# GpSimd takes two of the eight chunks of the residual update of a 512-token stage, from an SBUF copy of the norm factor

## The chip, the cores and the metric

The kernel runs on one NeuronCore of a Trainium2 chip (trn2). The metric is the device time of one execution in microseconds, the median of several runs. The engines are named as the profile names them: PE is TensorE, DVE is VectorE, ACT is ScalarE, POOL is GpSimd, SP is SyncE.

## The reference: what is computed

The program is a stack of two models in fp32. The part that the change touches is the end of the two branches of the first model's first layer, where a branch's output y is normalised, scaled and added to the stream x. In NumPy form (the token dimension holds 256 context and 256 latent tokens, which have different gains):

```
y = branch(x)                      # hybrid attention, then the feed-forward net
f = 1 / sqrt(mean(y * y over the 1024 features) + eps)       # one factor per token
x = x + gain[feature, context or latent] * (y * f)           # residual
f2 = 1 / sqrt(mean(x * x) + eps)                             # the next norm follows at once
h = gain2 * (x * f2) + shift2                                # input of the next products
```

The gains and shifts are modulation values: they come from products of a condition vector with a large weight, `ada_w`, which is streamed and multiplied throughout the first model.

## The kernel before, in words

Features lie on the 128 partitions in eight chunks, and tokens along the free axis. So x and y are the SBUF tiles `X` and `Y` of [128, 8, 512], and one chunk is 128x512. The program is written engine by engine, each a fixed list of instructions with hand-placed semaphores; nothing reorders it.

Large products run on PE with every operand split into a high and a low part, three matmuls for one (L458 to L460). For that, ACT copies each weight slot into its high part (L385) and DVE subtracts to get the low part `w_lo` (L395).

The residual of a 512-token stage is done twice, at the end of the hybrid branch (r = 0) and of the feed-forward branch (r = 1). These are its steps.

- ACT squares the chunks of `Y` as they are finished (L1008), POOL adds the first six squares (`pool_y_sum`), and PE sums over the partitions (`pe_residual`).
- ACT takes the root (L1032), DVE the reciprocal (L1040), and PE spreads the result over all partitions into a PSUM bank, `wk[:, 1, :]` (L739). This is the factor f.
- `dve_residual`: for each of the eight chunks DVE makes `nt = Y * f` over 512 columns (L1055, `Y` from SBUF and the factor from PSUM). Then come two instructions of 256 columns, one for each kind of token, `X = nt * gain + X` (L1049, `nt` and `X` both from SBUF). The product of chunk c + 1 stands ahead of the update of chunk c.
- The next norm follows the chunks. ACT squares `X[c]` (L767) when chunk c is updated, and PE adds the squares (L734). In between, PE multiplies the streamed modulation weights (L551), and after the squares of chunks 3, 5 and 7 ACT issues the DMA for the ring slot that PE has used up (L572; the ring has three slots of 1 MB). After the eighth square come the root (L772), the reciprocal (L793), the spread (L739), and DVE's `nt = X * f2` (L809).
- Before ACT can make the first normed chunk (L782), it has to take over the row of modulation results (L569), for which PE must have multiplied the last ring slot (L551).

POOL has nothing to do from its last addition of squares to the feed-forward net's gating, where it multiplies (L1125, L1126) and subtracts (L1128) tiles of 128x512 in SBUF.

Of the kernel before, what the change touches and what calls it, by code (L numbers as in the profile page):

```python
# [20 lines left out]
ALU = mybir.AluOpType  # L21
ACT = mybir.ActivationFunctionType
AX = mybir.AxisListType

P = 128
D = 1024
DC = D // P
# [144 lines left out]
def stack_kernel(nc, t, out, layers):  # L172
# [3 lines left out]
    with ctx:  # L176
# [51 lines left out]
        nt = at("nt", [P, 2, T1], nt0 + 10 * KB)  # L228
        n32 = at("n32", [P, 2, T1], nt0 + 14 * KB)

        ada_first = [at(f"ada_first{i}", [P, SLOT], o) for i, o in enumerate(
# [87 lines left out]
        def sem(name):  # L319
            sems[name] = ctx.enter_context(nc.semaphore(name))  # L320
            return sems[name]
# [381 lines left out]
        mh_mul, mh_done = sem("mlp_products"), sem("mlp_hidden_done")  # L703
        x_ready = sem("x_ready")
        s_meta = sem("meta_loaded")

        def x_ready_for(eng, j, c):
            if j == 0:
                eng.wait_ge(s_x, 16)
            elif j <= 4:  # L710
                eng.wait_ge(x_ready, 8 * (j - 1) + c + 1)
            else:
                if j == 7:
                    if c % 4 < 2:
                        eng.wait_ge(x_ready, 4 * DC + c // 4 + 1)
                    else:
                        eng.wait_ge(freed["dve"], proj["c_outb"].freed0 + c // 4 + 1)
                    return
                p = proj[("ab_out1", "mlp0_out1", None, "mlp1_out1")[j - 5]]
                eng.wait_ge(freed["dve"], p.freed0 + c // p.C + 1)  # L720
            if j == 4:
                eng.wait_ge(s_meta, 5 * 16)
# [162 lines left out]

        s_sum, n32_ctx = sem("first_square_sum"), sem("norm_out_first_half")

        def pe_first_norm(pe):
            pe.wait_ge(s_const, N_CONST)
            pe.wait_ge(nsq_used, DC)  # L890
            pe.matmul(wk[:, 0, :], ones[:, :], sq_acc[:, :], start=True, stop=True).then_inc(s_sum, 1)

        def act_first_norm(act):
# [16 lines left out]
            for c in range(DC):  # L910
                if c >= 2:
                    act.wait_ge(nsq_used, max(c - 1, 2))
                act.activation(sq[:, c % 2, :], X[:, c, :], ACT.Square).then_inc(nsq_ready, 1)
            act.wait_ge(s_sum, 1)
            act.activation(root[:, :], wk[:, 0, :], ACT.Sqrt, bias=V("eps"), scale=1.0 / D).then_inc(root_ready, 1)
# [112 lines left out]
        def act_residual(act, r):  # L1028
# [3 lines left out]
            act.activation(root[:, 0:w], wk[:, 1, 0:w], ACT.Sqrt, bias=V("eps"), scale=1.0 / D).then_inc(yroot_ready, 1)  # L1032

        def dve_residual(dve, r):
            n, x0, groups, (layer, j), _ = RES[r]
            dve.wait_ge(s_gain, (5, 7, 8, 9)[r])
            dve.wait_ge(yroot_ready, r + 1)
            w = P if n == T1 else n
            by = wk[:, 1, 0:n] if n == T1 else rstd[:, 0:n]
            dve.reciprocal(rstd[:, 0:w], root[:, 0:w]).then_inc(yrstd_ready, 1)  # L1040
            if n == T1:
                dve.wait_ge(spread, 2 * r + 1)
            else:
                dve.wait_ge(yrstd_ready, r + 1)

            def update(c):
                dve.wait_ge(yt_ready, DC * r + c + 1)
                for s, a, b in groups:
                    ins = dve.scalar_tensor_tensor(X[:, c, x0 + a:x0 + b], nt[:, c % 2, a:b], gains[:, layer, j, s, c:c + 1],  # L1049
                                                   X[:, c, x0 + a:x0 + b], ALU.mult, ALU.add)  # L1050
                ins.then_inc(x_ready, 1)
            for c in range(DC):
                if c >= 2:
                    dve.wait_ge(x_ready, DC * r + c - 1)
                dve.tensor_tensor(nt[:, c % 2, 0:n], Y[:, c, 0:n], by, ALU.mult).then_inc(yt_ready, 1)  # L1055
                if c >= 1:
                    update(c - 1)
                if r == 3 and c >= 2:
                    dve_scaled(dve, 4, c - 2)
            update(DC - 1)  # L1060
            if r == 3:
                for c in (DC - 2, DC - 1):
                    dve_scaled(dve, 4, c)
# [1755 lines left out]
        def act_ffn(act, layer, r):  # L2819
# [13 lines left out]
            act_residual(act, r)  # L2833
            if layer == 0:
                act_ada(act, ADA_FIRST + ADA_LATE + 2, ADA_FIRST + ADA_LATE + 4)

# [15 lines left out]
        def pool_ffn(pool, layer, r):  # L2852
            if layer == 0:
                pool_ffn_in(pool, layer, 0)
                pool_ffn_in(pool, layer, 1)
            pool_y_sum(pool, r)

        def pe_ffn_halves(pe, layer, j):
# [43 lines left out]
        def _(act):  # L2902
# [8 lines left out]
            act_ada(act, ADA_FIRST + ADA_OUT, ADA_FIRST + ADA_OUT + 2)  # L2911
            act_residual(act, 0)
            act_ada(act, ADA_FIRST + ADA_OUT + 2, ADA_FIRST + ADA_OUT + 4)
            act_norm(act, 1, meanwhile=lambda: act_ada(act, ADA_FIRST + ADA_OUT + 7, ADA_FIRST + ADA_OUT + 9),
# [78 lines left out]
        def _(pool):  # L2993
# [3 lines left out]
            pool_rpb(pool, link)  # L2997
            pool_y_sum(pool, 0)
            pool_ffn(pool, 0, 1)
            pool_ret(pool)  # L3000
# [215 lines left out]
```

## Time and profile before

| | |
|---|---|
| median of 3 runs | 2021.95 us (2020.9 to 2023.43) |
| the profiled execution's own time | 2020.81 us |
| its span in the profile | 2019.1 us |
| PE busy | 1921.5 us (95%) |
| DVE busy | 1243.1 us (62%) |
| ACT busy | 920.0 us (46%) |
| POOL busy | 217.6 us (11%) |
| DVE, 273 to 286 us (first residual) | 11.31 us of 13 |
| DVE, 675 to 689 us (second residual) | 11.74 us of 14 |

The span runs from the first to the last instruction. The profiled execution took 1.7 us more than it, and the median of the runs lies 1.1 us above the profiled execution. A busy share is an average over stages: the two residuals together are a little over 1% of the time, and what limits them must be read there.

### The profile page before, as it was taken

Reading aid. Unit: us, or ns where it says so; the run is one execution under the profiler, and the core shown is the slowest. Engines: PE = TensorE matmul, PEld = TensorE weight load, DVE = VectorE, ACT = ScalarE, POOL = GpSimd, SP = SyncE. Lnnn points to the kernel's source line nnn. Section 1 sums busy time; section 2 is a strip of 40 time slices with the busy share of each in tenths; the row PEclk is TensorE's granted clock in tenths of the full one; section 3 lists DMA queues with packets and bytes.
Section 4 is the critical chain, followed back from the end, with each engine's and each line's share of the span. In section 5 each row is a group of like instructions: output and inputs, shape, how many; then the busy total and the mean of one; then the engine's idle time right before and its main releaser. Section 6 shows DMA issues by size and latency. Waiting matters only on the chain.

```text
span 2019.1 us, 33489 instructions
## 1 busy us (share of the span) xinstructions
PE 1921.5 (95%) x13389; PEld 1710.9 (85%) x13389; DVE 1243.1 (62%) x1853; ACT 920.0 (46%) x1438; POOL 217.6 (11%) x171
## 2 busy tenths in 40 slices
PE   4999989999999899999899998999999999989998
PEld 3776657778888589999889997998899999879997
DVE  6355455543564546577577767656975557787564
ACT  4344344322332522177465554357554444655353
POOL 2100104430552000011000000000000010000001
PEclk8999989999999899999989999999999999999999
DMA  8621465433223433222444553532345453225553
GB/s 358 247 78 63 149 247 179 169 114 112 99 75 107 167 125 108 102 84 84 167 158 167 198 178 126 177 134 87 127 171 184 167 179 135 95 95 181 185 177 125
DMA packets 43951, 296.79 MB, mean 147 GB/s; under 512 B 4976, under 2 KB 6128, under 8 KB 11696
## 3 DMA queue, kind: packets, MB, share of 16 engines
q1 hardware_dynamic: 36576, 247.48, 35.3%
q10 hardware_dynamic: 6048, 42.50, 5.8%
q0 software_dynamic: 1200, 5.02, 0.7%
q8 instruction: 91, 1.49, 0.3%
q14 instruction: 36, 0.29, 0.0%
HBM read 293.94 MB, written 1.05 MB: 146 GB/s over the span
## 4 chain that ended last, share of the span: by engine, by line
PE 84%; DVE 8%; ACT 4%; issue 1%; DMA 1%; POOL 1%; SPq 0%; ACTq 0%; DVEq 0%; POOLq 0%
PE acc L458 23%; PE acc L460 23%; PE acc L459 23%; DVE w_lo L395 2%; PE acc L453 2%; PE acc L455 2%; PE acc L454 2%; PE wk L551 1%; PE wk L1709 1%; DMA ada_first<-in_w_ada 1%; ACT w_hi L385 1%; PE acc L1698 1%; DVE X L1049 1%; PE wk L1438 1%; DVE nt L1055 1%
## 5 line engine op out<-in xcount | busy, mean ns | idle before, releaser
L395 DVE TENSOR_TENSOR w_lo<-w_raw,w_hi 128x1024 fp32r<-128x1024 f32 (+2 forms) x472 | 575.1, 1257 | 179.8 <-ACT w_hi L385 178.3
L458 PE MATMUL acc<-Hhi,w_hi 128*128 128x272 f32 (+2 forms) x2048 | 656.0, 320 | 24.8 <-DVE Hlo L804 7.6
L385 ACT ACTIVATE w_hi<-w_raw 128x1024 fp32r<-128x1024 f32 (+2 forms) x472 | 452.4, 1005 | 431.0 <-PE acc L460 346.4
L460 PE MATMUL acc<-Hhi,w_lo 128*128 128x272 f32 (+2 forms) x2048 | 637.9, 311 | 0.0
L459 PE MATMUL acc<-Hlo,w_hi 128*128 128x272 f32 (+2 forms) x2048 | 637.2, 311 | 0.0
L458 PEld LDWEIGHTS acc<-Hhi,w_hi 128*128 128x128 f32 x2048 | 388.6, 190 | 71.2 <-issue 38.7
L460 PEld LDWEIGHTS acc<-Hhi,w_lo 128*128 128x128 f32 x2048 | 388.4, 190 | 19.7
L459 PEld LDWEIGHTS acc<-Hlo,w_hi 128*128 128x128 f32 x2048 | 388.6, 190 | 18.0
L458 PE MATMUL acc<-Fhi,w_hi 128*128 128x256 f32 (+2 forms) x864 | 263.8, 305 | 3.0 <-POOL Flo L1128 1.5
L460 PE MATMUL acc<-Fhi,w_lo 128*128 128x256 f32 (+2 forms) x864 | 263.4, 305 | 0.0
L459 PE MATMUL acc<-Flo,w_hi 128*128 128x256 f32 (+2 forms) x864 | 263.1, 304 | 0.0
L458 PEld LDWEIGHTS acc<-Fhi,w_hi 128*128 128x128 f32 x864 | 162.4, 188 | 11.7 <-POOL Flo L1128 2.4
L460 PEld LDWEIGHTS acc<-Fhi,w_lo 128*128 128x128 f32 x864 | 162.5, 188 | 7.0
L459 PEld LDWEIGHTS acc<-Flo,w_hi 128*128 128x128 f32 x864 | 162.2, 188 | 6.6
L1084 ACT ACTIVATE cgu<-acc,vec 128x512 f32<-128x512 f32 x44 | 34.2, 779 | 125.6 <-PE acc L460 125.6
L1106 DVE SCALAR_TENSOR_TENSOR cgu<-acc,vec,cgu 128x510 f32<-128x510 f32 x44 | 32.6, 743 | 88.7 <-ACT cgu L1084 88.7
L458 PE MATMUL acc<-Rhi,w_hi 128*128 128x256 f32 (+1 forms) x256 | 84.3, 329 | 2.0 <-DVE Rlo L804 1.8
L460 PE MATMUL acc<-Rhi,w_lo 128*128 128x256 f32 (+1 forms) x256 | 79.3, 310 | 0.0
L459 PE MATMUL acc<-Rlo,w_hi 128*128 128x256 f32 (+1 forms) x256 | 79.2, 310 | 0.0
L453 PE MATMUL acc<-w_hi,Rhi 128*128 128x256 f32 x256 | 72.1, 282 | 0.0
L454 PE MATMUL acc<-w_lo,Rhi 128*128 128x256 f32 x256 | 70.7, 276 | 0.0
L455 PE MATMUL acc<-w_hi,Rlo 128*128 128x256 f32 x256 | 70.7, 276 | 0.0
(413 smaller groups left out, 2667.6 us busy)
## 6 DMA issues: line engine op xcount, KB each, us to landing
w_raw<-in_w_ffn_in SPq DMA_DIRECT2D x44, 1024.0 KB, 4.8
ada_ring<-in_w_ada ACTq DMA_DIRECT2D x40, 1024.0 KB, 6.0
w_raw<-in_w_mlp_in SPq DMA_DIRECT2D x32, 1024.0 KB, 4.8
w_raw<-in_w_mlp_out SPq DMA_DIRECT2D x32, 1024.0 KB, 4.8
w_raw<-in_w_ffn_out SPq DMA_DIRECT2D x32, 704.0 KB, 4.1
ada_first<-in_w_ada SPq DMA_DIRECT2D x8, 1024.0 KB, 18.2
w_raw<-in_w_ret_v SPq DMA_DIRECT2D x8, 1024.0 KB, 4.8
w_raw<-in_w_ret_g SPq DMA_DIRECT2D x8, 1024.0 KB, 4.8
```

The lines of the kernel that those rows point to most:

```text
L385: act.activation(w_hi[:, r, a:b], w_raw[:, r, a:b], ACT.Copy).then_inc(hi_done, 1)
L395: dve.tensor_tensor(w_lo[:, r, a:b], w_raw[:, r, a:b], w_hi[:, r, a:b].bitcast(F32), ALU.subtract).then_inc(lo_done, 1)
L453: pe.matmul(o, x_hi(k)[:, toks], w_hi[:, r, w], start=k == 0, stop=False)
L454: pe.matmul(o, x_hi(k)[:, toks], w_lo[:, r, w], start=False, stop=False)
L455: mm = pe.matmul(o, x_lo(k)[:, toks], w_hi[:, r, w], start=False, stop=k == last)
L458: pe.matmul(o, w_hi[:, r, w], x_hi(k), start=k == 0, stop=False)
L459: pe.matmul(o, w_hi[:, r, w], x_lo(k), start=False, stop=False)
L460: mm = pe.matmul(o, w_lo[:, r, w], x_hi(k), start=False, stop=k == last)
L551: mm = pe.matmul(wk[b:b + 32, bank, 0:256], cvec[:, k, 30 - 2 * j:62 - 2 * j], w[:, k * 256:(k + 1) * 256], start=first and k < 4, stop=la ...
L1049: ins = dve.scalar_tensor_tensor(X[:, c, x0 + a:x0 + b], nt[:, c % 2, a:b], gains[:, layer, j, s, c:c + 1], X[:, c, x0 + a:x0 + b], ALU.mu ...
L1084: act.activation(cgu[:, r, c, 0:n], acc_tile(p, r, c), ACT.Identity, bias=Vd("conv_b", m + layer * 44), scale=Vd("conv_w", m + (layer * 3 ...
L1106: dve.scalar_tensor_tensor(seqs(o, 1, SEQ), seqs(acc_tile(p, r, c), 0, SEQ - 1), w, seqs(o, 1, SEQ), ALU.mult, ALU.add).then_inc(conv_left, 1)
```

## The change

In both 512-token residuals, chunks 0 to 5 stay with DVE, and chunks 6 and 7 go to POOL. POOL has no path to PSUM in this program, so ACT first copies the factor from PSUM to a new SBUF tile `fac` (`act_factor`). DVE now reads `fac` too, not the PSUM bank. POOL does a chunk in four instructions: `nt_pool = Y * fac` over 512 columns, two products with the gains over 256 columns each, and `X = X + nt_pool` over 512 columns. The semaphore values that wait for an updated chunk are counted anew, since POOL's chunks report on a semaphore of their own. The 256-token residuals (r = 2, 3) stay as they were.

```diff
+        fac = at("fac", [P, T1], A + 20 * KB)
+        nt_pool = at("nt_pool", [P, 2, T1], A + 22 * KB)
...
+        POOL_C = (6, 7)
+        x_ready, pool_steps = sem("x_ready"), sem("first_sum_then_residual_steps_of_pool")
+        PER = 1 + 3 * len(POOL_C)
+        X_BASE = [0, DC - len(POOL_C), 2 * (DC - len(POOL_C)), 3 * DC - 2 * len(POOL_C), 4 * DC - 2 * len(POOL_C)]
...
             elif j <= 4:
-                eng.wait_ge(x_ready, 8 * (j - 1) + c + 1)
+                if j <= 2 and c in POOL_C:
+                    eng.wait_ge(pool_steps, PER * (j - 1) + 3 * POOL_C.index(c) + 5)
+                else:
+                    eng.wait_ge(x_ready, X_BASE[j - 1] + c + 1)
...
+        def act_factor(act, r):
+            act.wait_ge(spread, 2 * r + 1)
+            act.activation(fac[:, :], wk[:, 1, :], ACT.Copy).then_inc(pool_steps, 1)
+
+        def pool_residual(pool, r):
+            n, x0, groups, (layer, j), _ = RES[r]
+            pool.wait_ge(s_gain, (5, 7)[r])
+            pool.wait_ge(pool_steps, PER * r + 2)
+            for i, c in enumerate(POOL_C):
+                pool.tensor_tensor(nt_pool[:, i, :], Y[:, c, :], fac[:, :], ALU.mult).then_inc(pool_steps, 1)
+                pool.wait_ge(pool_steps, PER * r + 3 * i + 3)
+                for q, a, b in groups:
+                    ins = pool.tensor_scalar(nt_pool[:, i, a:b], nt_pool[:, i, a:b], gains[:, layer, j, q, c:c + 1], None, ALU.mult)
+                ins.then_inc(pool_steps, 1)
+                pool.wait_ge(pool_steps, PER * r + 3 * i + 4)
+                pool.tensor_tensor(X[:, c, :], X[:, c, :], nt_pool[:, i, :], ALU.add).then_inc(pool_steps, 1)
...
         def dve_residual(dve, r):
...
-            by = wk[:, 1, 0:n] if n == T1 else rstd[:, 0:n]
+            by = fac[:, 0:n] if n == T1 else rstd[:, 0:n]
             dve.reciprocal(rstd[:, 0:w], root[:, 0:w]).then_inc(yrstd_ready, 1)
             if n == T1:
-                dve.wait_ge(spread, 2 * r + 1)
+                dve.wait_ge(pool_steps, PER * r + 2)
...
-            for c in range(DC):
+            last = X_BASE[r + 1] - X_BASE[r]
+            for c in range(last):
...
-            update(DC - 1)
+            update(last - 1)
...
             act_residual(act, r)
             if layer == 0:
+                act_factor(act, 1)
                 act_ada(act, ADA_FIRST + ADA_LATE + 2, ADA_FIRST + ADA_LATE + 4)
...
             pool_y_sum(pool, r)
+            if r == 1:
+                pool_residual(pool, r)
...
             act_residual(act, 0)
+            act_factor(act, 0)
             act_ada(act, ADA_FIRST + ADA_OUT + 2, ADA_FIRST + ADA_OUT + 4)
...
             pool_y_sum(pool, 0)
+            pool_residual(pool, 0)
             pool_ffn(pool, 0, 1)
```

On POOL, at the end of the hybrid branch, the list of before goes from the sums of squares straight to the gating of the feed-forward net:

```order
L1018 TENSOR_TENSOR sq_acc<-sq_acc,sq 128x512 [waits y_square_added,y_square_ready] x5
L1125 TENSOR_TENSOR hid<-sg,cgu 128x512 [waits silu_done,acc_freed_dve]
L1126 TENSOR_TENSOR Fhi_100<-sg,cgu 128x512
L1128 TENSOR_TENSOR Flo_103<-hid,Fhi_100 128x512 [waits hidden_product]
L1125 TENSOR_TENSOR hid<-sg,cgu 128x512 [waits silu_done,acc_freed_dve]
```

After the change eight instructions stand there, whose inputs are all in SBUF:

```order
L1026 TENSOR_TENSOR sq_acc<-sq_acc,sq 128x512 [waits y_square_added,y_square_ready] x5
L1051 TENSOR_TENSOR nt_pool<-Y,fac 128x512 [waits first_sum_then_residual_steps_of_pool,gains_ready]
L1054 TENSOR_SCALAR nt_pool<-nt_pool,gains 128x256 [waits first_sum_then_residual_steps_of_pool]
L1054 TENSOR_SCALAR nt_pool<-nt_pool,gains 128x256
L1057 TENSOR_TENSOR X<-X,nt_pool 128x512 [waits first_sum_then_residual_steps_of_pool]
L1051 TENSOR_TENSOR nt_pool<-Y,fac 128x512
L1054 TENSOR_SCALAR nt_pool<-nt_pool,gains 128x256 [waits first_sum_then_residual_steps_of_pool]
L1054 TENSOR_SCALAR nt_pool<-nt_pool,gains 128x256
L1057 TENSOR_TENSOR X<-X,nt_pool 128x512 [waits first_sum_then_residual_steps_of_pool]
L1151 TENSOR_TENSOR hid<-sg,cgu 128x512 [waits silu_done,acc_freed_dve]
```

The five sums ahead and the gating behind are as they were.

On DVE, at the end of the same residual, this is the list of before (the products of chunks 6 and 7 with the updates of chunks 5 to 7, then the next norm's reciprocal):

```order
L1055 TENSOR_TENSOR nt<-Y,wk 128x512 [waits x_ready]
L1049 SCALAR_TENSOR_TENSOR X<-nt,gains,X 128x256 [waits y_scaled_ready]
L1049 SCALAR_TENSOR_TENSOR X<-nt,gains,X 128x256
L1055 TENSOR_TENSOR nt<-Y,wk 128x512 [waits x_ready]
L1049 SCALAR_TENSOR_TENSOR X<-nt,gains,X 128x256 [waits y_scaled_ready]
L1049 SCALAR_TENSOR_TENSOR X<-nt,gains,X 128x256
L1049 SCALAR_TENSOR_TENSOR X<-nt,gains,X 128x256 [waits y_scaled_ready]
L1049 SCALAR_TENSOR_TENSOR X<-nt,gains,X 128x256
L793 RECIPROCAL rstd<-root 128x128 [waits norm_root_ready]
```

And this is the list after the change, from the product of chunk 5 on:

```order
L1081 TENSOR_TENSOR nt<-Y,fac 128x512 [waits x_ready]
L1074 SCALAR_TENSOR_TENSOR X<-nt,gains,X 128x256 [waits y_scaled_ready]
L1074 SCALAR_TENSOR_TENSOR X<-nt,gains,X 128x256
L1074 SCALAR_TENSOR_TENSOR X<-nt,gains,X 128x256 [waits y_scaled_ready]
L1074 SCALAR_TENSOR_TENSOR X<-nt,gains,X 128x256
L801 RECIPROCAL rstd<-root 128x128 [waits norm_root_ready]
```

Two chunks (six instructions) are gone, and the second operand of every `nt` product is `fac` in SBUF where it was `wk` in PSUM.

On ACT, between the root of y and the squares of the next norm, the list of before is:

```order
L1032 ACTIVATE root<-wk,vec 128x128 [waits y_square_added]
L572 DMA ada_ring<-in_w_ada 128x2048 [waits ada_slot_used] x2
L767 ACTIVATE sq<-X 128x512 [waits x_ready] x2
L767 ACTIVATE sq<-X 128x512 [waits norm_square_summed,x_ready] x2
L572 DMA ada_ring<-in_w_ada 128x2048 [waits ada_slot_used]
```

After the change it is:

```order
L1040 ACTIVATE root<-wk,vec 128x128 [waits y_square_added]
L1044 ACTIVATE fac<-wk 128x512 [waits rstd_spread]
L574 DMA ada_ring<-in_w_ada 128x2048 [waits ada_slot_used] x2
L775 ACTIVATE sq<-X 128x512 [waits x_ready] x2
L775 ACTIVATE sq<-X 128x512 [waits norm_square_summed,x_ready] x2
L574 DMA ada_ring<-in_w_ada 128x2048 [waits ada_slot_used]
```

The copy of the factor stands ahead of two ring DMAs, and waits for PE's spread.

## Rows read from the trace of the kernel before

**Rows 1.** The page, part 4: the whole chain by engine.

```profile
PE 84%; DVE 8%; ACT 4%; issue 1%; DMA 1%; POOL 1%; SPq 0%; ACTq 0%; DVEq 0%; POOLq 0%
```

**Rows 2.** Chain of waits, first residual: start us, us, what.

```profile
272.57 1.29 DVE nt L1055 x2
...
282.25 0.69 DVE nt L1055
...
282.94 1.60 DVE X L1049 x4
...
285.24 0.47 PE wk L734 x8
...
285.73 0.38 ACT root L772
...
287.14 1.16 PE wk L739 x8
...
288.33 1.11 PE wk L551 x16
```

**Rows 3.** Timeline, first residual: start us, us, engine, line, op, names, [idle before].

```profile
269.31 0.33 ACTq L572 DMA_DIRECT2D ada_ring<-in_w_ada  x1
...
281.35 0.87 DVE L1049 SCALAR_TENSOR_TENSOR X<-nt,gains,X 128x256 f32<-128x256 f32 x2
...
282.26 0.33 ACTq L572 DMA_DIRECT2D ada_ring<-in_w_ada  x1
...
283.18 1.05 PE L551 MATMUL wk<-ada_ring,cvec 128*32 128x256 f32 x16
...
288.33 0.59 PEld L551 LDWEIGHTS wk<-ada_ring,cvec 128*32 128x32 f32 x16 [0.22 <-DMA ada_ring<-in_w_ada]
```

**Rows 4.** Timeline, second residual.

```profile
684.59 0.88 DVE L1049 SCALAR_TENSOR_TENSOR X<-nt,gains,X 128x256 f32<-128x256 f32 x2
...
685.58 0.34 ACTq L572 DMA_DIRECT2D ada_ring<-in_w_ada  x1
...
689.04 0.37 ACT L772 ACTIVATE root<-wk,vec 128x128 f32<-128x128 f32 x1 [0.61 <-PE wk L734]
...
691.53 1.07 PE L551 MATMUL wk<-ada_ring,cvec 128*32 128x256 f32 x16
```

**Rows 5.** Groups of instructions by line and shape: count, busy us, mean ns, idle.

```profile
L1125 POOL TENSOR_TENSOR hid<-sg,cgu 128x512 f32<-128x512 f32 x22 | 28.5, 1296 | 234.6 <-ACT sg L1088 234.6
...
L1018 POOL TENSOR_TENSOR sq_acc<-sq_acc,sq 128x256 f32<-128x256 f32 x10 | 7.4, 740 | 41.0 <-ACT sq L1008 41.0
...
L1015 POOL COPY sq_acc<-sq 128x256 f32<-128x256 f32 x2 | 0.8, 398 | 181.6 <-ACT sq L1008 181.6
...
L767 ACT ACTIVATE sq<-X 128x512 f32<-128x512 f32 x16 | 10.1, 630 | 19.8 <-DVE X L1049 14.5 <-PE wk L551 5.2
...
L1049 DVE SCALAR_TENSOR_TENSOR X<-nt,gains,X 128x256 f32<-128x256 f32 x48 | 21.4, 478 | 0.0
...
L1084 ACT ACTIVATE cgu<-acc,vec 128x512 f32<-128x512 f32 x44 | 34.2, 779 | 125.6 <-PE acc L460 125.6
```

**Rows 6.** Timelines: POOL and DVE in the feed-forward loop; DVE alone later.

```profile
333.44 1.31 POOL L1125 TENSOR_TENSOR hid<-sg,cgu 128x512 f32<-128x512 f32 x1 [6.53 <-ACT sg L1088]
...
334.70 2.27 POOL L1126 TENSOR_TENSOR Fhi<-sg,cgu 128x512 f32 x1
...
337.14 2.08 POOL L1128 TENSOR_TENSOR Flo<-hid,Fhi 128x512 f32 x1 [0.17 <-POOL Fhi L1126]
...
334.25 3.80 DVE L395 TENSOR_TENSOR w_lo<-w_raw,w_hi 128x1024 fp32r<-128x1024 f32 x2 [0.99 <-ACT w_hi L385]
...
1459.92 2.36 DVE L395 TENSOR_TENSOR w_lo<-w_raw,w_hi 128x1024 fp32r<-128x1024 f32 x2 [0.71 <-ACT w_hi L385]
```

**Rows 7.** Timelines: DVE and POOL in a later norm.

```profile
1822.92 4.79 DVE L834 SCALAR_TENSOR_TENSOR Hlo<-X,vec,Hhi 128x256 fp32r<-128x256 f32 x7
...
1823.37 3.66 POOL L845 TENSOR_TENSOR sq_acc<-sq_acc,sq 128x256 f32<-128x256 f32 x4 [0.59 <-ACT sq L828]
```

More of the change, by code:

```diff
@@ L703, in stack_kernel @@
         mh_mul, mh_done = sem("mlp_products"), sem("mlp_hidden_done")
-        x_ready = sem("x_ready")
+        POOL_C = (6, 7)
+        x_ready, pool_steps = sem("x_ready"), sem("first_sum_then_residual_steps_of_pool")
+        PER = 1 + 3 * len(POOL_C)
+        X_BASE = [0, DC - len(POOL_C), 2 * (DC - len(POOL_C)), 3 * DC - 2 * len(POOL_C), 4 * DC - 2 * len(POOL_C)]
         s_meta = sem("meta_loaded")
@@ L714, in x_ready_for @@
                     if c % 4 < 2:
-                        eng.wait_ge(x_ready, 4 * DC + c // 4 + 1)
+                        eng.wait_ge(x_ready, X_BASE[4] + c // 4 + 1)
                     else:
@@ L884, in final_norm @@
                         .then_inc(mh_done if by_pool else n32_ready, 1)
-        s_sum, n32_ctx = sem("first_square_sum"), sem("norm_out_first_half")
+        n32_ctx = sem("norm_out_first_half")
         def pe_first_norm(pe):
@@ L890, in pe_first_norm @@
             pe.wait_ge(nsq_used, DC)
-            pe.matmul(wk[:, 0, :], ones[:, :], sq_acc[:, :], start=True, stop=True).then_inc(s_sum, 1)
+            pe.matmul(wk[:, 0, :], ones[:, :], sq_acc[:, :], start=True, stop=True).then_inc(pool_steps, 1)
         def act_first_norm(act):
@@ L913, in act_first_norm @@
                 act.activation(sq[:, c % 2, :], X[:, c, :], ACT.Square).then_inc(nsq_ready, 1)
-            act.wait_ge(s_sum, 1)
+            act.wait_ge(pool_steps, 1)
             act.activation(root[:, :], wk[:, 0, :], ACT.Sqrt, bias=V("eps"), scale=1.0 / D).then_inc(root_ready, 1)
@@ L1046, in update @@
             def update(c):
-                dve.wait_ge(yt_ready, DC * r + c + 1)
+                dve.wait_ge(yt_ready, X_BASE[r] + c + 1)
                 for s, a, b in groups:
@@ L1051, in update @@
                 ins.then_inc(x_ready, 1)
-            for c in range(DC):
+            last = X_BASE[r + 1] - X_BASE[r]
+            for c in range(last):
                 if c >= 2:
-                    dve.wait_ge(x_ready, DC * r + c - 1)
+                    dve.wait_ge(x_ready, X_BASE[r] + c - 1)
                 dve.tensor_tensor(nt[:, c % 2, 0:n], Y[:, c, 0:n], by, ALU.mult).then_inc(yt_ready, 1)
```

## The prediction

> **What bounds the kernel now.** I read the page's chain first: PE holds 84% of it, DVE 8% and ACT 4% [rows 1]. An average over 2 ms says nothing on a step of 12 us, so next came the chain of waits in the first residual. There DVE holds it alone, from the first product at 272.57 to the last update at 284.54, in steps of one product (0.69) and two updates (0.80 together), about 1.5 us a chunk. After the last update come one square, one sum (285.24), the root (285.73), the reciprocal and spread (287.14 to 288.30), and then modulation products of PE at 288.33 [rows 2]. Third, the timeline: those products did not start by themselves. Their weights came from a ring DMA issued at 282.26, right when ACT squared chunk 5, and PE's weight load shows the DMA as its releaser at 288.33 [rows 3]. So two chains end together at 288.3: the residual's, and a DMA that starts when chunk 5 is updated. In the second residual the same two are there: chunk 5 updated at 685.47, DMA issued at 685.58, root at 689.04, products at 691.53 without a DMA wait [rows 4].
>
> I name the time at which chunk 5 is updated T5: 281.35 + 0.87 = 282.22 before.
>
> **What the change removes.** DVE loses two chunks, 3.0 us. Only the product of chunk 6 (0.69) stood ahead of T5; the rest (2.3) stood behind it. What now follows T5: PE's modulation products end 2.0 behind it (283.18 + 1.05 against 282.22 [rows 3]), and the two last sums need 0.47 each [rows 2]. They can't start before, since PE runs in order. So the root comes at T5 + 2.9, where it came at T5 + 3.5 (285.73). Of 3.0 us removed, 0.6 plus the 0.69 can be had.
>
> **What it adds ahead of DVE.** DVE now waits for ACT's copy of the factor, 128x512. A square of that size from SBUF takes 0.630, an instruction with scale and bias from PSUM 0.779 [rows 5]; I take 0.65 with the hand-over, near the plain one, which eats the 0.69. At the upper bound both residuals are 0.13 later. DVE's first product starts at 273.2. Six chunks alone take 282.22 - 272.57 - 0.69 = 9.0, so T5 without any disturbance is 282.2, as before.
>
> ACT's copy also holds back the ring DMA of 269.31 [rows 3] by about 3.9 us, to 273.2. With the 6.07 us from issue to use of the row at 282.26 it is there by 279.3; its slot is multiplied behind chunk 3, two chunks (3.0) ahead of 283.18, at 280.2 or later. Hidden by 0.9 us; if that cover fails, PE is late by what is missing. Behind DVE's and POOL's new waits nothing else is queued that could have run: POOL's next work is the gating, some 20 us later.
>
> **What POOL costs.** Per residual it does four instructions of 128x512 with two tensor inputs, and four products of 128x256 with one tensor input and a gain. The first kind takes 1.296 alone, 1.26 from start to start [rows 5, 6]. The second kind is not in this trace. Its bounds are a copy of 128x256 (0.398) and a two-input instruction of that size (0.740) [rows 5]; it has one tensor input, so I take 0.45, near the copy. Alone POOL needs 4 x 1.26 + 4 x 0.45 + 0.3 for its own waits = 7.1 us. It would be done at 280.4, well ahead of ACT's need for chunk 6.
>
> The Trainium skill, GPSIMD Engine Reference, section Engine selection, says that one-input elementwise work is roughly at line rate on GpSimd and two-input work about twice as slow as on VectorE. By it the gain product would be the copy's, and the sum below 0.4 us lower over both residuals; no run here shows it yet.
>
> **What the two engines do to each other.** This is the term that decides. In the feed-forward loop POOL's three instructions, 1.3 each, took 1.31, 2.27 and 2.08 when DVE's pair of `w_lo` subtractions (both inputs in SBUF) fell among them, and that pair took 3.80, where the same pair alone takes 2.36 [rows 6]. Both sides lost: DVE 1.44. They took turns: what DVE lost is the rest of `hid` (334.25 to 334.74, 0.49) and all of `Fhi` (1.25), less 0.1 at each of three changes of turn. The updates of the residual are of another opcode, so I looked for one of its form. In a later norm seven such (SBUF, pointer, SBUF, 128x256) took 4.79 while POOL added squares [rows 7]. Alone they take 6 x 0.40 + 0.48 = 2.9 [rows 2, 5]. DVE lost 1.9 to four POOL instructions of 0.740, 0.48 each: again the length less about 0.25. So each POOL instruction costs a busy DVE its own length less 0.2.
>
> Before the change the product took its factor from PSUM. Now `nt = Y * fac` has both inputs in SBUF, the form of `w_lo`, and the updates have the form just seen. Every DVE instruction of the residual can lose its turn, and DVE has 18 without a gap against POOL's 8. Loss: 4 x (1.26 - 0.2) + 4 x (0.45 - 0.2) = 5.2 us per residual. Bounds: with 0.4 instead of 0.2 for the turn, 4 x 0.86 + 4 x 0.05 = 3.6; with nothing for it and 0.740 for the products, 4 x 1.26 + 4 x 0.74 = 8.0.
>
> The Trainium skill, SBUF — State Buffer, section SBUF: two separate sides, calls the pair of ports that VectorE and GpSimd share an exclusive lock, taken by whichever starts first for the whole instruction, for VectorE instructions with two SBUF inputs as well. The trace agrees but for the 0.1 at each change of turn. With whole instructions the loss would be 4 x 1.296 + 4 x 0.45 = 7.0 and not 5.2.
>
> **The sum.** T5 becomes 282.2 + 5.2 = 287.4. POOL, with a DVE instruction between any two of its own, ends at about 283, so ACT doesn't wait for chunks 6 and 7. Root: 287.4 + 2.9 = 290.3, which is 4.6 later. The spread ends 2.57 behind it, at 292.9. The ring DMA is issued at 287.4 and with the same 6.07 is there at 293.5, 5.2 later than before; it may land sooner than before, with less behind it in the queue, so I take the middle, +4.9. Second residual: T5 690.7, root 693.6, +4.6, and its DMA had at most 5.95 (685.58 to 691.53), so it stays near the spread. Together +9.5 us: 2020.81 + 9.5 = 2030.3. The median of the runs lies 1.1 above the profiled execution, so I predict 2031. From the bounds: 3.6 gives 2 x 3.0 = +6.0 (2028 as a median), 8.0 gives about 2 x 7.6 = +15.2 (2037).
>
> **Rivals.**
> - *No collision.* T5 stays 282.2, POOL ends at 280.4. The root comes 0.6 earlier, but the ring DMA still leaves at 282.3 and is there at 288.3, so the first residual gains nothing; the second gains 0.6 at most. Median 2021.3 to 2022: no change. It decides if this DVE form doesn't give way to POOL. For it: no row has this very pair of instructions. Against it: [rows 6, 7] have both forms losing. Chance 0.1.
> - *POOL starves.* DVE keeps its turn from one instruction to the next, T5 is 282.2 and POOL does its 7.1 us behind it, to 289.3. Then a square and a sum (0.63 + 0.47): root 290.4, +4.7 each, the DMA hidden. 2020.8 + 9.4, as a median 2031. Against it: POOL got its turns in both rows. It is the same time with another picture. Chance 0.1.
> - *Whole instructions.* DVE loses 7.0, T5 is 289.2, root +6.4, the first DMA up to +7.0: about +13.1, median 2035. It is what the skill's rule gives. For it: POOL's 1.8 us lost in [rows 6] to two `w_lo` is nearly all of their 2.36. Chance 0.15.
> - *Faster after all.* Everything behind T5 moves freely and ACT's copy is hidden: 2 x 3.0 less 2 x 0.65, -4.7, median 2017. The ring DMA in [rows 3] speaks against it. Chance 0.02.
> - My forecast, +6 to +12: 0.6. The last 0.03 is left to a cover that fails (the held-back DMA), slower than all these.
>
> **How the numbers follow.** About 0.2% (4 us) is what a measurement of this kernel can tell from no change. Slower by more: forecast 0.6, starvation 0.1, whole instructions 0.15, the last 0.03, less 0.01 for a forecast that ends short: 0.87. Same: 0.11. Faster: 0.02. The time is that of the forecast, 2031. The range goes from 2027 (a little under the lower bound) to 2036, which takes in the rule's 2035 and leaves out the no-collision case.
>
> **What would show it.** Right: in the first residual `nt` products of DVE with a mean over 0.9 where they had 0.69, updates over 0.48 while POOL is busy, POOL's 128x512 over 1.6, T5 near 287, ACT idle ahead of the square of chunk 5 for DVE and not for POOL, root near 290. The time lost stands between 273 and 293 and again between 676 and 697, and nothing elsewhere. Wrong: DVE at its old lengths with POOL running beside it (no collision), or POOL's eight instructions behind DVE's last (starvation); a gain product on POOL over 0.74; or a slower stretch that neither residual holds.

## The result, and the profile after

The changed kernel takes 2031.71 us (median of 6 runs, 2027.89 to 2034.52); the kernel before takes 2023.05 us (6 runs, 2020.9 to 2024.35). The ratio is 1.0043, with a 95% interval of 1.0031 to 1.0056. That is 8.7 us slower (6.3 to 11.3). The forecast was 2031. Of all runs in this document one stands apart: one of the twelve runs of the kernel with POOL on two columns took 3812 us, and it is left out of that kernel's ratio.

The profiled execution after has a span of 2030.8 us, 11.7 more than the one before. Of these, 2.0 us were lost before the first residual, where no instruction of the engines' work is changed. The root of y comes at 271.89 there and at 269.90 before; in the ten other traces, with and without POOL's chunks, it comes at 269.66 to 271.45. So this part is spread between executions. The chain by engine is the same as in [rows 1], to the per cent, so the page doesn't show the loss. The chain of waits in the first residual shows it (start us, us, what):

```profile
274.56 0.61 ACT fac L1044
...
275.19 2.37 DVE nt L1081 x2
...
286.66 0.64 ACT sq L775
...
288.00 1.71 PE wk L553 x16
289.71 0.85 PE wk L742 x16
290.56 1.71 PE wk L553 x16
292.27 0.90 PE wk L742 x16
...
293.19 0.38 ACT root L780
...
295.75 1.04 PE wk L553 x16
```

Against [rows 2], ACT's copy of the factor has come into the chain. Two products of DVE that took 1.29 now take 2.37. And at the end the chain no longer runs through DVE's last update. It leaves DVE at the update of chunk 3, whose square starts at 286.66, and from 287.34 on it stays with PE, which needs 1.71 in the chain, twice, for modulation products between two sums. The timeline of the same stretch shows who ran beside whom (start us, us, engine, line, operation):

```profile
281.29 1.65 DVE L1081 TENSOR_TENSOR nt<-Y,fac 128x512 f32<-128x512 f32 x1
...
282.49 2.25 POOL L1054 TENSOR_SCALAR nt_pool<-nt_pool,gains 128x256 f32<-128x256 f32 x2
...
284.82 1.53 POOL L1057 TENSOR_TENSOR X<-X,nt_pool 128x512 f32<-128x512 f32 x1
...
286.66 0.69 DVE L1081 TENSOR_TENSOR nt<-Y,fac 128x512 f32<-128x512 f32 x1
...
287.27 1.67 DVE L1074 SCALAR_TENSOR_TENSOR X<-nt,gains,X 128x256 f32<-128x256 f32 x4
...
289.77 0.34 ACTq L574 DMA_DIRECT2D ada_ring<-in_w_ada  x1
...
290.33 1.93 PE L553 MATMUL wk<-ada_ring,cvec 128*32 128x256 f32 x16
```

POOL is done at 286.35, and DVE's next product is at once back at 0.69. Chunk 5 is updated at 288.94 (287.27 + 1.67). The modulation products of PE take 1.93, where [rows 3] had 1.05. The groups of the whole trace say how much longer each kind has become (count | busy us, mean ns | idle):

```profile
L1074 DVE SCALAR_TENSOR_TENSOR X<-nt,gains,X 128x256 f32<-128x256 f32 x40 | 22.8, 599 | 0.0
L1081 DVE TENSOR_TENSOR nt<-Y,fac 128x512 f32<-128x512 f32 x12 | 12.8, 1081 | 4.0 <-ACT fac L1044 3.8
...
L1054 POOL TENSOR_SCALAR nt_pool<-nt_pool,gains 128x256 f32<-128x256 f32 x8 | 9.0, 1133 | 0.4
...
L1051 POOL TENSOR_TENSOR nt_pool<-Y,fac 128x512 f32<-128x512 f32 x4 | 6.3, 1579 | 33.8 <-ACT fac L1044 33.8
L1057 POOL TENSOR_TENSOR X<-X,nt_pool 128x512 f32<-128x512 f32 x4 | 6.1, 1525 | 0.3
```

Both engines lost. The updates were 478 ns [rows 5] and the products 0.69 us [rows 2]. Per residual the loss is 40 x (0.599 - 0.478) / 2 = 2.4 us for the updates and 12 x (1.081 - 0.69) / 2 = 2.35 us for the products, 4.75 together. (The group of updates has in both kernels 16 instructions of the 256-token residuals, which are not changed; they drop out of the difference.)

This table splits each residual at the same marks, read from the timelines (us; first / second residual). "DVE" is from its first product to its last update, "tail" from there to the next norm's root, and "all" from the root of y to ACT taking over the modulation row, the last thing that the next stage needs.

| kernel | root of y to first product | DVE | tail | root to root | all |
|---|---|---|---|---|---|
| before (T5 at 9.65) | 2.67 | 11.96 / 11.95 | 1.20 / 1.27 | 15.83 / 15.89 | 19.57 / 19.57 |
| after | 3.30 | 13.75 / 13.74 | 4.25 / 3.29 | 21.30 / 20.33 | 24.93 / 24.01 |
| factor in PSUM | 3.30 | 11.38 / 11.37 | 3.46 / 3.58 | 18.14 / 18.25 | 21.77 / 21.93 |
| one after the other | 12.46 | 8.95 / 8.96 | 2.69 / 2.57 | 24.10 / 23.98 | 30.25 / 28.02 |
| POOL on 2 columns | 3.30 | 9.00 / 8.98 | 3.01 / 3.00 | 15.31 / 15.28 | 20.03 / 19.15 |
| gain products only | 3.30 | 9.70 / 9.71 | 2.51 / 2.79 | 15.51 / 15.80 | 20.80 / 19.60 |
| two-input ones only | 3.30 | 13.02 / 13.01 | 3.03 / 4.24 | 19.35 / 20.55 | 23.96 / 24.24 |
| one chunk | 3.30 | 12.92 / 12.91 | 1.73 / 1.79 | 17.95 / 18.00 | 22.46 / 21.68 |
| one chunk, PSUM | 3.30 | 10.96 / 10.96 | 1.72 / 1.79 | 15.98 / 16.05 | 20.52 / 19.73 |
| PE kept busy | 3.84 / 3.30 | 13.78 / 13.75 | 2.50 / 2.58 | 20.12 / 19.63 | 23.93 / 24.76 |
| ACT makes the gain product, first run | 2.67 | 10.44 / 10.44 | 1.21 / 1.27 | 14.32 / 14.39 | 24.01 / 18.07 |
| ACT makes the gain product, second run | 2.67 | 10.44 / 10.42 | 1.82 / 1.28 | 14.93 / 14.37 | 18.61 / 18.05 |

The two residuals cost 5.4 and 4.4 us more than before, 9.8 together. With the 2.0 of the opening, and -0.3 and +0.2 between and behind them, that is the 11.7 of the spans.

### The profile page after: what moved, and what is told of

It reads as the page before. It is cut to its first block, busy times and chain, and to the rows that moved or that the text cites. A ratio compares the mean times of both kernels' runs of the same rounds, so it can differ in the third digit from the quotient of the medians.

```text
span 2030.8 us, 33497 instructions
## 1 busy us (share of the span) xinstructions
PE 1925.7 (95%) x13389; PEld 1712.8 (84%) x13389; DVE 1248.0 (61%) x1841; ACT 920.8 (45%) x1440; POOL 237.9 (12%) x187
## 3 DMA queue, kind: packets, MB, share of 16 engines
HBM read 293.94 MB, written 1.05 MB: 145 GB/s over the span
## 4 chain that ended last, share of the span: by engine, by line
PE 84%; DVE 8%; ACT 4%; issue 1%; DMA 1%; POOL 1%; SPq 0%; ACTq 0%; DVEq 0%; POOLq 0%
PE acc L460 23%; PE acc L462 22%; PE acc L461 22%; PE acc L455 2%; DVE w_lo L397 2%; PE acc L457 2%; PE acc L456 2%; PE wk L553 2%; DMA ada_first<-in_w_ada 1%; PE wk L1735 1%; ACT w_hi L387 1%; PE acc L1724 1%; DVE nt L1081 1%; PE wk L1464 1%; DVE X L1074 1%
## 5 line engine op out<-in xcount | busy, mean ns | idle before, releaser
L460 PEld LDWEIGHTS acc<-Fhi,w_hi 128*128 128x128 f32 x864 | 162.3, 188 | 11.3 <-issue 2.2
```

Of the source, the lines that this page charges most:

```text
L460: pe.matmul(o, w_hi[:, r, w], x_hi(k), start=k == 0, stop=False)
```

## The experiments

Four questions were open: whether POOL and DVE really take turns and at what price for each kind of instruction; what the copy and the held-back DMA cost by themselves; why the tail is longer than forecast; and whether there is a form that wins.

**The factor from PSUM for DVE.** ACT still makes `fac`, and POOL reads it; DVE's products read the PSUM bank again.

```diff
-            by = fac[:, 0:n] if n == T1 else rstd[:, 0:n]
+            by = wk[:, 1, 0:n] if n == T1 else rstd[:, 0:n]
```

> DVE still waits for the copy of the factor, but its products read the factor from PSUM again, so only its updates have two SBUF inputs. Turns (my theory: an instruction of POOL and one of DVE with two SBUF inputs exclude each other): each of the products, 0.61 to 0.69 long, now runs beside POOL, so DVE loses less than the 4.75 us of the changed kernel. From the first product to the update of chunk 5 it takes about 12 us, not 13.75, all products have 0.69, and the time is some 3 us under the changed kernel, still 5 over the kernel before. Rival (any DVE instruction gives way to POOL, whatever it reads): 13.75 us again, products of 0.85 to 1.76, and the changed kernel's time. Rival (the copy and the ring DMA held back behind it cost the time, not the collisions): the changed kernel's time too, with short products.

Measured: 2027.9 us (before 2021.55), ratio 1.0034, 1.0021 to 1.0047. The groups of its trace:

```profile
L1074 DVE SCALAR_TENSOR_TENSOR X<-nt,gains,X 128x256 f32<-128x256 f32 x40 | 22.8, 599 | 0.0
...
L1081 DVE TENSOR_TENSOR nt<-Y,wk 128x512 f32<-128x512 f32 x12 | 8.1, 686 | 4.0 <-ACT fac L1044 3.8
L1054 POOL TENSOR_SCALAR nt_pool<-nt_pool,gains 128x256 f32<-128x256 f32 x8 | 8.0, 1005 | 0.4
```

The products are at 0.69 although POOL runs beside them, and the updates are as long as in the changed kernel. The loss of DVE is 11.38 - 9.0 = 2.4, the share of the updates alone. So the second input in SBUF is what makes a product give way to POOL, and half of the collision was brought in by `fac`. What keeps this kernel slower is the other half, the 0.63 of the copy, and a tail of 3.5.

**POOL on two columns.** All eight POOL instructions stay, each of two columns or one, and the rest of chunks 6 and 7 is not computed.

```diff
-                pool.tensor_tensor(nt_pool[:, i, :], Y[:, c, :], fac[:, :], ALU.mult)...
+                pool.tensor_tensor(nt_pool[:, i, 0:2], Y[:, c, 0:2], fac[:, 0:2], ALU.mult)...
-                for q, a, b in groups:
+                for q, a, b in [(1, 0, 1), (1, 1, 2)]:
-                pool.tensor_tensor(X[:, c, :], X[:, c, :], nt_pool[:, i, :], ALU.add)...
+                pool.tensor_tensor(X[:, c, 0:2], X[:, c, 0:2], nt_pool[:, i, 0:2], ALU.add)...
```

> POOL's instructions stay in number and order but work on two columns each, so most of the update of chunks 6 and 7 is left out. All waits, the copy of the factor and the held-back ring DMA stay. Turns: DVE is at its own speed, 9.0 us from the first product to the update of chunk 5 with at most 1 us lost to eight short POOL instructions; the root of the next norm comes 0 to 0.6 us earlier than before, and the time is that of the kernel before within 2 us (2021 to 2025). Rival (copy and held-back DMA cost the time): it stays 5 us or more above the kernel before, with PE waiting for the DMA.

Measured: 2021.86 us (before 2021.55), ratio 1.0001, 0.9992 to 1.0011. DVE takes 9.0 for six chunks, as read from [rows 2]: the collision is all of DVE's loss. But even here, with two chunks gone for nothing, the kernel is not faster. The root comes 0.5 earlier than before in the first residual, and the modulation row 0.46 later. PE's timeline there:

```profile
280.79 1.93 PE L553 MATMUL wk<-ada_ring,cvec 128*32 128x256 f32 x16
...
286.38 1.16 PE L747 MATMUL wk<-rstd,ident 128*128 128x128 f32 x8 [0.61 <-DVE rstd L801]
288.55 1.07 PE L553 MATMUL wk<-ada_ring,cvec 128*32 128x256 f32 x16 [1.01 <-DMA ada_ring<-in_w_ada]
```

PE stood 1.01 for the ring DMA, the second chain of [rows 3]. ACT issued that DMA at 282.79, not when chunk 5 was updated (281.96) but when the slot came free: PE's products of 280.79 took 1.93, at a granted clock of 0.61 in the mean from 280 to 284, and ended at 282.72. The second residual gains 0.4. Even so this tail is 3.0 where the kernel before had 1.2: the time that DVE saves is mostly spent behind it.

**Which POOL instructions cost what.** In one kernel only the gain products are whole, in the other only the two-input instructions; the others are cut to one or two columns.

```diff
 (gain products only; both two-input instructions cut to two columns as above)
-                    ins = pool.tensor_scalar(nt_pool[:, i, a:b], nt_pool[:, i, a:b], gains[...], None, ALU.mult)
+                    ins = pool.tensor_scalar(nt_pool[:, i, a:b], Y[:, c, a:b], gains[...], None, ALU.mult)
 (two-input ones only)
-                for q, a, b in groups:
+                for q, a, b in [(1, 0, 1), (1, 1, 2)]:
```

> The changed kernel with POOL's instructions of 128x512 cut to two columns and its gain products whole (most of the update of chunks 6 and 7 is left out). In e4 a gain product alone took 0.91 us, over my bound of 0.74, yet DVE lost only about 0.2 to each. If the hold on DVE is the reading of the tensor and not the length of the instruction, DVE loses 4 x 0.2 = 0.8 here: 9.8 us from the first product to its last update. Rival (a gain product holds DVE for its whole length): 4 x 0.9 = 3.6, so 12.6 us.

> The other half: POOL's four instructions of 128x512 with two inputs whole, the gain products on one column each (the gains of chunks 6 and 7 are left out). If each costs DVE 1.0 to 1.06, DVE loses 4.0 to 4.2: 13.0 to 13.2 us from the first product to its last update, where the changed kernel has 13.75. Rival (the loss goes with the count of POOL instructions and the turns between them): as in the changed kernel, 13.75.

Measured, one run each: 2026.23 and 2032.65 us. The times of single runs say little, the traces much. DVE and POOL with gain products only:

```profile
278.88 2.38 POOL L1054 TENSOR_SCALAR nt_pool<-Y,gains 128x256 f32<-128x256 f32 x2
...
279.37 1.09 DVE L1074 SCALAR_TENSOR_TENSOR X<-nt,gains,X 128x256 f32<-128x256 f32 x2
280.50 0.85 DVE L1081 TENSOR_TENSOR nt<-Y,fac 128x512 f32<-128x512 f32 x1
281.27 0.87 DVE L1074 SCALAR_TENSOR_TENSOR X<-nt,gains,X 128x256 f32<-128x256 f32 x2
```

Four gain products cost DVE 9.70 - 9.00 = 0.7, in steps of 0.22 (a pair of updates at 1.09 for 0.87) and 0.16 (a product at 0.85 for 0.69): 0.18 each, though each is 0.92 long alone and 1.17 beside DVE here. With the two-input instructions only:

```profile
276.94 0.88 DVE L1074 SCALAR_TENSOR_TENSOR X<-nt,gains,X 128x256 f32<-128x256 f32 x2
277.85 1.64 DVE L1081 TENSOR_TENSOR nt<-Y,fac 128x512 f32<-128x512 f32 x1
279.42 1.88 DVE L1074 SCALAR_TENSOR_TENSOR X<-nt,gains,X 128x256 f32<-128x256 f32 x2
```

Here a collision costs 0.95 to 1.01, and four of them 13.02 - 9.00 = 4.0. The sum of the parts, 4.7, is the 4.75 of the changed kernel.

**One after the other.** DVE begins only when POOL has finished both chunks.

```diff
-                dve.wait_ge(pool_steps, PER * r + 2)
+                dve.wait_ge(pool_steps, PER * r + 3 * len(POOL_C) + 2)
```

> DVE waits until POOL has done its two chunks, so neither disturbs the other: the price of each alone. POOL's instructions of 128x512 take 1.29 each, the gain products of 128x256 are near the copy's 0.40 (0.45 expected, 0.74 at most), together 7.1 us; then DVE's six chunks take 9.0 with products of 0.69, although they read both inputs from SBUF. If the products had over 0.8 here, the SBUF copy itself would be the slow source and not POOL. The update of chunk 5 comes at 16.1 us behind the copy, 2.4 later than in the changed kernel; with two residuals the time is about 2036.

Measured: 2041.74 us (one run). The groups:

```profile
L1081 DVE TENSOR_TENSOR nt<-Y,fac 128x512 f32<-128x512 f32 x12 | 8.1, 691 | 22.3 <-POOL X L1057 22.1
L1054 POOL TENSOR_SCALAR nt_pool<-nt_pool,gains 128x256 f32<-128x256 f32 x8 | 7.3, 921 | 0.4
...
L1051 POOL TENSOR_TENSOR nt_pool<-Y,fac 128x512 f32<-128x512 f32 x4 | 5.0, 1262 | 33.4 <-ACT fac L1044 33.4
L1057 POOL TENSOR_TENSOR X<-X,nt_pool 128x512 f32<-128x512 f32 x4 | 5.0, 1260 | 0.3
```

DVE's products with `fac` in SBUF are 0.69 when POOL is silent. POOL alone takes 9.0 us (274.12 to 283.14), not the 7.1 of the prediction. The 128x512 are 1.26 as forecast; the gain products are 0.92, where 0.45 was assumed. Those 1.9 us in each residual are most of what the run lies above its expectation.

**One chunk on POOL**, with the factor from SBUF and from PSUM.

```diff
-        POOL_C = (6, 7)
+        POOL_C = (7,)
 (the second kernel also)
-            by = fac[:, 0:n] if n == T1 else rstd[:, 0:n]
+            by = wk[:, 1, 0:n] if n == T1 else rstd[:, 0:n]
```

> POOL gets only chunk 7, DVE seven chunks. Turns: the loss goes with the number of POOL instructions, four and not eight, so DVE loses about 2.4 us per residual, and chunk 6 costs it 1.5 again. Update of chunk 5 at 9.65 + 2.4 = 12.05 us behind the first product, update of chunk 6 at 12.9; the root about 3 us later than before per residual, the time 5 to 6 us above the kernel before. Rival (a fixed cost of using POOL at all, as the copy, the wake-up or the DMA held back): the time of the changed kernel, 8 to 9 us above.

> The kindest form of the change: POOL has chunk 7 alone, and DVE's products read the factor from PSUM. By the turns DVE loses half of what e1 lost, 1.2 us, and has seven chunks: 10.5 + 1.2 = 11.7 us, from a start that is 0.63 later for ACT's copy. So DVE's end is 0.4 later than before, and ACT and PE follow it with less: from the root of y to the next row of modulation results 19.6 to 20.3 us, where before had 19.57; the time is 0 to 2 us over the kernel before, no change. If it were clearly faster, POOL could pay after all, and my reading that the copy and the turns eat all of it would be wrong.

Measured: 2027.13 us, ratio 1.003 (1.0018 to 1.0041), and 2023.61 us, ratio 1.0007 (0.9997 to 1.0017). With half the POOL instructions the loss up to chunk 5 is half, 12.1 - 9.65 = 2.5. With the factor in PSUM as well, DVE's seven chunks take 10.96 for 10.5 undisturbed, and the kernel can't be told from the one before. The expectation had a loss of 1.2, half of the 2.4 with two chunks, and 0.5 came. POOL's first product falls on DVE's products here as there, and they lose nothing. With one chunk its gain products cost 0.22 and its addition 0.30 (a pair of updates at 1.17 for 0.87). With two chunks and the factor in PSUM its first addition and its second product both fall on one pair of updates (2.19 for 0.87), and its last addition on the last four (2.37 for 1.67). So the price goes by which DVE instruction a POOL instruction meets, and not by the count of POOL's instructions alone. What is left to win goes to the ring DMA again: PE waited 0.83 for it in the first residual.

**PE kept busy.** In the changed kernel, six small products of no use stand ahead of the sums of chunks 0, 1 and 3, to see whether PE's idle time between chunks lengthens the tail.

```diff
+                if j in (1, 2) and c in (0, 1, 3):
+                    for _ in range(6):
+                        pe.matmul(acc[:, 0, 0:P], ones[:, :], ones[:, :], start=True, stop=True)
                 pe.wait_ge(nsq_ready, DC * j + c + 1)
```

> The changed kernel with six idle-time matmuls (ones by ones, 128 columns, into an unused PSUM tile) on PE ahead of the squares of chunks 0, 1 and 3 in both norms, where PE otherwise waits about 2 us for each chunk. In the changed kernel the next root comes 4.25 and 3.29 us behind DVE's last update, where I had 2.9, and the modulation products there take 1.93 and not 1.05. If that is PE at its lower clock after the idle waits (my theory), the products behind chunks 3 and 5 take 1.05 to 1.1, the root comes 2.7 to 3.0 us behind DVE's last update in both, DVE's 13.75 stays, and the time is 1 to 2 us under the changed kernel. Rival (the products wait for their weights or for ACT, not for the clock): they keep 1.93 or the root keeps its 4.25 and 3.29.

Measured: 2031.54 us (before 2022.86), ratio 1.0046, 1.0029 to 1.0062. The 1 to 2 us that were expected under the changed kernel did not come. The stretches of the first residual in the kernel before (PE, PEld, DVE, ACT and POOL busy, then PEclk, the granted clock; 1.00 is 2.4 GHz and 0.50 is 1.2 GHz):

```profile
276.00:280.00 4.00, 3.53 (x44) 1.68 (x48) 3.90 (x9) 1.99 (x4) 0.00 (x0) 0.51 0.84 317
280.00:284.00 4.00, 2.69 (x56) 1.33 (x56) 3.93 (x9) 1.50 (x3) 0.00 (x0) 1.00 0.93 317
```

in the changed kernel:

```profile
276.00:280.00 4.00, 1.92 (x24) 0.42 (x12) 3.96 (x6) 0.63 (x1) 3.81 (x4) 0.50 0.91 332
280.00:284.00 4.00, 2.03 (x24) 0.99 (x24) 3.93 (x5) 0.65 (x2) 3.90 (x4) 0.50 0.49 197
284.00:288.00 4.00, 1.65 (x24) 0.80 (x24) 3.96 (x6) 1.24 (x2) 2.26 (x2) 0.50 0.19 27
288.00:292.00 4.00, 4.00 (x48) 2.17 (x44) 0.94 (x3) 2.41 (x4) 0.00 (x0) 0.50 0.88 301
```

and with the filler:

```profile
280.00:284.00 4.00, 3.32 (x45) 2.24 (x44) 3.97 (x4) 0.63 (x1) 3.90 (x4) 0.98 0.59 244
284.00:288.00 4.00, 2.51 (x36) 2.04 (x40) 3.93 (x7) 1.26 (x2) 2.37 (x2) 1.00 0.26 39
288.00:292.00 4.00, 3.29 (x72) 1.73 (x68) 1.09 (x4) 2.78 (x5) 0.00 (x0) 1.00 0.85 348
```

The cause of the long tail is shown: the clock is at 0.98 to 1.00 from 280 on, the modulation products are back at 1.05, and the tail is 2.50 and 2.58 instead of 4.25 and 3.29. But only the first residual is shorter, by 1.0. (Its 3.84 to the first product is not the filler's: PE's spread, ahead of any filler, took 1.70 for 1.16.) In the second the root is 0.7 earlier and the modulation row 0.75 later. PE's timeline in the second residual:

```profile
699.17 1.07 PE L553 MATMUL wk<-ada_ring,cvec 128*32 128x256 f32 x16 [0.26 <-DMA ada_ring<-in_w_ada]
700.45 1.16 PE L747 MATMUL wk<-rstd,ident 128*128 128x128 f32 x8 [0.21 <-DVE rstd L804]
702.99 1.07 PE L553 MATMUL wk<-ada_ring,cvec 128*32 128x256 f32 x16 [1.38 <-DMA ada_ring<-in_w_ada]
```

The DMA was issued at 696.51, landed 6.4 later and was used 6.48 later. In the changed kernel the same DMA was issued at 698.07, landed 4.8 later, 0.2 ahead of its use, and held nothing up. So a shorter tail uncovers the DMA, as in the kernel with two columns, but that is not all of it: the DMA also took 1.6 longer. It was issued 2.31 behind the ring DMA before it, where the changed kernel had 3.10; whether that is the cause, no run shows.

**The gain product on ACT.** This one starts from the kernel before. ACT is idle while Y is finished, so it multiplies `Y` by the gain there, behind the squares, and the last chunks behind the root. DVE's update becomes one plain addition of 128x512, and POOL has no part in it.

```diff
+        def act_gain(act, r, m):
+            n, x0, groups, (layer, j), _ = RES[r]
+            act.wait_ge(ysq_ready, DC * r + m + 1)
+            for s, a, b in groups:
+                ins = act.activation(Y[:, m, a:b], Y[:, m, a:b], ACT.Identity, scale=gains[:, layer, j, s, m:m + 1])
+            ins.then_inc(y_gained, 1)
...
+                if r < 2:
+                    dve.tensor_tensor(X[:, c, :], X[:, c, :], nt[:, c % 2, :], ALU.add).then_inc(x_ready, 1)
+                    return
```

> From the kernel before, without POOL and without a copy of the factor: ACT multiplies each chunk of Y by its gain in place, behind its square, in time in which it is idle; DVE's residual is then nt = Y * f and one X = X + nt over 512 columns where it had two instructions of 256. If DVE's chain is what the residual lasts (my theory), a chunk takes 1.31 and not 1.51 us, eight chunks 10.4 and not 11.95, and from the root of y to the next row of modulation results it is about 18.1 us, not 19.57, in both residuals: 2.5 to 3 us less in all, some 0.13%, at the edge of what the runs can tell. Rival (the ring DMA that leaves when chunk 5 is updated sets the end): the first residual gains what chunk 5 gains, 1.1, the second 1.4. Rival (the longer ACT list delays the squares or the root): the stretch from Y to the root grows by 1 us or more and the gain is gone.

> The kernel of e5 once more, for one thing: in the profile of e5 PE waited 3.9 us in the first residual for a ring DMA, and the gain of 1.5 us in DVE's chain was lost there five-fold, though the median was 1.7 us better. If the wait is of one execution, this profile has about 18.1 to 18.5 us from the root of y to the modulation row in the first residual, as in the second, and the time is again some 0.1% under the kernel before. If the earlier chain always outruns the ring there, the wait of several us is here again.

Measured: 2020.16 us (before 2021.85), ratio 0.9989, 0.998 to 0.9997; and again 2021.82 us (before 2022.86), ratio 0.9992, 0.9982 to 1.0001. DVE's timeline in the second run:

```profile
281.28 0.68 DVE L1064 TENSOR_TENSOR X<-X,nt 128x512 f32<-128x512 f32 x1
282.00 0.69 DVE L1075 TENSOR_TENSOR nt<-Y,wk 128x512 f32<-128x512 f32 x1
282.61 1.29 DVE L1064 TENSOR_TENSOR X<-X,nt 128x512 f32<-128x512 f32 x2
```

One update takes 0.68, where the pair took 0.87 [rows 3], and all eight chunks 10.44 instead of 11.96. The residuals are 1.0 and 1.5 us shorter. In the profile of the first run PE stood 3.88 for the ring DMA in the first residual, which made that residual 4.4 us longer than before. The DMA issued at 279.95 took 8.9 us to land; in the repetition the same one, issued at 279.36, took 5.0 and PE didn't wait, so that stall belongs to one execution. Why it was slow there, the traces don't show. This kernel beats the changed one by about 10 us. Over the kernel before its gain is 1 to 2 us, at the edge of what the runs can tell.

## Why the prediction was right

- **What DVE loses to POOL.** Forecast 5.2 us per residual, measured 4.75. The mechanism is shown three ways: it is gone with two columns, half gone with half the instructions, and gone for the products alone when their factor is in PSUM. Half the instructions with the factor in PSUM cost a fifth and not half, so the forecast's count of instructions holds only where every DVE instruction can lose its turn.
- **The two-input term** was 4 x 1.06 = 4.2 and measured 4.0. The rule read from [rows 6, 7], the length less 0.2, held for them.
- **The gain term** was 4 x (0.45 - 0.2) = 1.0 and measured 0.7, by two errors that nearly cancelled. The instruction takes 0.92, outside the bounds of 0.398 and 0.740. And DVE loses 0.18 to it, not its length less 0.2, which would be 0.7. The bounds came from instructions without a gain pointer; the nearest rows were not near.
- **The start of DVE.** Forecast 0.65 later by the copy, measured 0.63 (3.30 against 2.67). Its six chunks alone were 9.0, as forecast.
- **The tail was mis-sized, and its path was another.** The step failed where the prediction says "PE's modulation products end 2.0 behind" T5, and the root at T5 + 2.9. It came at 4.25 and 3.29 behind. The 1.05 for the modulation products was read from [rows 3], at the full clock. In the changed kernel PE idles 2.0 us ahead of three of the first four sums (those of chunks 0, 1 and 3), the granted clock is 0.50 from 276 to 292 (before it was back at 1.00 from 280 on), and the products take 1.93. With them PE has no idle time from the sum of chunk 3 to the root, so in the first residual the root hangs on chunk 3 and not on T5. The filler shows the clock as the cause. The kernel before already had such products in the same residual, at a granted clock of 0.51:

```profile
277.30 1.93 PE L551 MATMUL wk<-ada_ring,cvec 128*32 128x256 f32 x16
```

- **The ring DMA.** Forecast was an issue at T5 and use 6.07 later, behind the spread; it was issued at 289.77, 0.8 behind T5, because the slow products released the slot at 289.70, and used 5.91 later. It had landed 0.1 ahead of that and the products followed the spread, so PE did not wait for it, where the forecast had the DMA end last. The DMA that ACT's copy held back was hidden, as forecast: issued at 274.57, it landed 6.2 later, and its weights were multiplied at 287.77. The modulation row of the first residual is 5.4 later (forecast 4.9), that of the second 4.4 (forecast 4.6). The sum is 9.8 for 9.5, and that closeness is partly luck: DVE lost 0.45 less than forecast in each residual, and the tails were 1.35 and 0.4 longer. The medians differ by 8.7, where the forecast of 2031 lies 9.1 above the 2021.95 from which it was reckoned.
- **POOL's end.** Alone 9.0 and not 7.1; beside DVE 11.05, to 286.35, where the prediction had about 9.8. That is still 2.6 ahead of DVE's last update, so ACT never waited for it, and the error cost nothing.
- **The signs that were named.** Products over 0.9 (1.08), and updates over 0.48, came as said. "POOL's 128x512 over 1.6" did not: they are 1.55 in the mean. "A gain product on POOL over 0.74" was named as a sign against the forecast. It came, and its error was undone by the other.
- **The rivals.** *No collision* falls with the 1081 ns of the products. *POOL starves* falls with POOL's rows: it got its turns and ended first. *Whole instructions* had 7.0 lost in each residual, and 4.75 were; it is nearer for the two-input kind (1.0 of 1.26 lost) and wrong for the gain products (0.18 of 0.92). *Faster after all* falls with the kernel of two columns: without any collision it is no faster than before. How much of that is the lower clock, which kept its ring slot busy longer, and how much the copy, is not shown; no kernel has both the two columns and the filler.

## What to carry to other kernels

Before work is moved to an idle GpSimd, ask whether both engines will have all their inputs in SBUF at that time: each two-input instruction of GpSimd then takes most of its own length from VectorE (1.0 of 1.26 us here), and offloading two chunks of eight cost 4.75 us where they had taken 3.0. An operand left in PSUM keeps that instruction out of it. And when the engine that sets the pace gets slower, PE idles longer between its small products and does them at the lower clock, so durations read at the full clock are too short there (1.05 for 1.93); before counting a gain in such a tail, look for the DMA that ends within a microsecond of it.

## What the runs showed of the hardware that was not expected

- A GpSimd product with one tensor input and a gain pointer takes 0.92 us for 128x256, more than the two-input instruction of that size (0.740, [rows 5]) and over twice the copy (0.398). Cut to one column it still takes 0.5 us, where a two-input instruction cut to two columns took 0.19 to 0.22, and 0.64 only as the first behind the wait:

```profile
275.36 0.99 POOL L1054 TENSOR_SCALAR nt_pool<-nt_pool,gains 128x1 f32<-128x1 f32 x2
```

  The Trainium skill, GPSIMD Engine Reference, section Engine selection, has one-input work at roughly line rate and two-input work slower. For this product the trace doesn't agree, and the measurement decides.
- Yet it costs VectorE only about 0.2 us, while a two-input one of 1.26 costs 1.0. Why it costs so little for its length, no run shows.
- A VectorE product with one input in PSUM and one in SBUF lost nothing to GpSimd (686 ns beside it). One with both in SBUF did, and so did the updates, whose third operand is a pointer. The Trainium skill, SBUF — State Buffer, section SBUF: two separate sides, says that a GpSimd instruction and a VectorE instruction with two SBUF inputs want the same pair of ports, and that whichever starts first has it for its whole instruction while the other blocks. The trace agrees on which VectorE instructions are concerned. On how long it agrees within 0.3 us for the two-input instructions of GpSimd, and not for the gain product.
- Neither engine starved: wherever both were busy, each got a turn within an instruction or two of the other. Both were slowed; POOL's eight instructions took 9.0 us alone and 11.05 beside VectorE.
- The time from issue to landing of a ring DMA of 1 MB at one place of the program is not fixed: 8.9 us and 5.0 in two executions of the last kernel, in the first residual, and in the second residual 4.8 in the changed kernel and 6.4 with the filler.
